# First head of the expert lookup scored by halves inside query unit 1, its first eight row numbers ahead of the rest, query units 2 to 4 unsplit

## The chip, the cores and the metric

One core of a Trainium2 chip runs the whole program. The metric is the device time of one execution in microseconds (us); smaller is better. The engines are TensorE (PE in the profile, with PEld for its weight loads), VectorE (DVE), ScalarE (ACT), GpSimd (POOL) and SyncE (SP); 16 DMA engines move the data.

## What is computed

Two transformer blocks over 256 tokens of width 1024, all in float32. The change lies in the last part, a feed-forward layer whose experts are looked up (PEER):

```python
def peer_ffn(x, w_q, sub_keys, u, v):
    def block(xb):                                   # 128 tokens
        q = (xb @ w_q).reshape(PEER_BLOCK, PEER_HEADS, 2, PEER_HALF)   # 8 heads, 2 halves of 128
        scores = jnp.einsum('thpd,hpkd->thpk', q, sub_keys).astype(jnp.float32)
        top_s, top_i = lax.top_k(scores, PEER_TOPK)  # 16 of 128 keys, for each half
        cand_s = (top_s[:, :, 0, :, None] + top_s[:, :, 1, None, :]).reshape(...)      # 16 x 16 sums
        cand_i = (top_i[:, :, 0, :, None] * PEER_N_KEYS + top_i[:, :, 1, None, :]).reshape(...)
        best_s, best_pos = lax.top_k(cand_s, PEER_TOPK)
        expert = jnp.take_along_axis(cand_i, best_pos, axis=-1)
        gate = jax.nn.softmax(best_s, axis=-1)
        act = jax.nn.gelu(jnp.einsum('thkd,td->thk', u[expert], xb).astype(jnp.float32), approximate=False)
        return jnp.einsum('thk,thkd->td', (gate * act).astype(v.dtype), v[expert])
```

## The kernel before

All matrices stream through nine raw buffers (`raw`, `RAW = 9`) in units of 128 x 1024 numbers, loaded by SyncE in a fixed order (line 572). A split unit is cut into a high part (`hi`, ScalarE, line 674) and a low part (`lo`, VectorE, line 1043), and TensorE multiplies each 128 x 128 piece three times (lines 548 to 550). Its raw buffer is free again after `lo`. A plain unit is multiplied as it lies in `raw` with the plain float32 activations `XF` (line 2269), and its buffer is free when TensorE has finished it. XF is written by ScalarE in eight copies, with one signal, `s_txf`, after the last (line 1015).

The order of the work on each engine is written out by hand, and each engine waits on semaphores. The lookup goes like this:

- TensorE forms the queries in 16 units `pq` 0 to 15, two for each head; ScalarE copies each to `QP` (line 1005). The units 0 to 4 are split, 5 to 15 plain. Units 0 to 15 lie in raw buffers 6, 7, 8, 0, 1, ..., 8, 0, 1, 2, 3, so unit 9 follows unit 0 in its buffer, unit 10 unit 1, and so on.
- A head's scores (line 2286: two halves times two token blocks, four matmuls, eight rows in the trace) follow a unit: head 0 after unit 1, head 1 after unit 4, head 2 after unit 6, and so on; ScalarE copies them to `SC` (line 1011).
- VectorE's `route` makes 16 row numbers of them for each token. `top16` (lines 1586 to 1593) is a search in five operations: the eight greatest, replace them, their places, the next eight, their places. It runs on both halves of 128 scores, then on the 256 sums (line 1608). Then shift, mask, convert (1616 to 1619), and for each half a comparison, a product and a sum over 256 elements (1621 to 1626) look up the key numbers; line 1629 writes the row numbers `EX`.
- GpSimd issues the gathers, one for each of 2 blocks x 8 heads x 16 (line 657). Gather g brings for each of the 128 tokens one row of 2048 numbers, the expert's u and v. It waits every 16 gathers for the head's row numbers (`s_exi`), for the landing of the gather 8 before (4 before, for the first 16), and for its buffer.
- There are 15 row buffers: four that are free early, then YH, YL, and halves of WH and WL (free after the last split unit), then pairs of raw buffers: 4-5 for the 11th gather (free after unit 8), 6-7 for the 15th (after unit 10), 0-1 for the 27th (after unit 13), and 2-3 and XF for the 35th and 36th (after unit 15). A used buffer is free again when TensorE has finished the slot of its gather.
- A slot: VectorE's dot product of u with the token (line 1669), ScalarE's gelu, gate and diagonal matrix (986 to 994), TensorE's product with v (line 2248, four rows in the trace). From unit 9 on, four slots follow each unit on TensorE (`MIX0 = 9`, `MIX = 4`); the other 228 follow unit 15.

Of the kernel before, what the change touches and what calls it, by code (L numbers as in the profile page):

```python
# [8 lines left out]
U32 = mybir.dt.uint32  # L9
# [5 lines left out]
T = 256  # L15
# [23 lines left out]
def plan():  # L39
# [97 lines left out]
    for t in range(16):  # L137
        add("pq", 1024, t < 5, lambda a, t=t: tile_b(a["peer_w_q_2"][0], ar(128) + 128 * t))
    return out
# [118 lines left out]
def program(nc, wst, cst, x, skt, uv, out, vscr, cscr, units):  # L258
    ctx = ExitStack()
    with ctx:  # L260
# [46 lines left out]
        def flat(ap):  # L307
# [130 lines left out]
        s_txf, s_xtt, s_qp, s_scm, s_scr = (sem(n) for n in ("x_gained", "x_turned", "pq_out", "pq_scores",  # L438
                                                                 "scores_out"))
        s_exi, s_bd, s_bde, s_gate, s_dot, s_gelu, s_wv, s_dg, s_y, s_ot, s_otd, s_left = (sem(n) for n in (  # L440
            "expert_index", "best_shifted", "best_exp", "gate", "dot", "gelu", "weight", "diag", "y_mm", "y_out", "y_out_right", "y_left_done"))
# [142 lines left out]
        def pool_program(po):  # L584
# [60 lines left out]
            for g in range(256):  # L645
                blk, s = g // 128, g % 128
                row, free, _ = rows[home[g]]
                if s % 16 == 0:
                    po.wait_ge(s_exi, g // 16 + 1)
                flying = FLYING // 2 if g < 2 * FLYING else FLYING  # L650
                if g >= flying:
                    po.wait_ge(s_g[home[g - flying]], 16 * turn_of[g - flying])
                if before[g] is None:
                    po.wait_ge(*free)
                else:
                    po.wait_ge(s_y, before[g] + 1)
                po.indirect_dma_start(row, None, uv if row.dtype == F32 else uv.bitcast(F32R), bass.IndirectOffsetOnAxis(ap=EX[:, blk, s:s + 1].bitcast(U32), axis=0)  # L657
                                      ).then_inc(s_g[home[g]], 16)


        def act_program(ac):
# [337 lines left out]
            for n in range(16):  # L999
# [3 lines left out]
                if n >= QN_RING:  # L1003
                    ac.wait_ge(s_scm, (n - QN_RING) // 2 + 1)
# [27 lines left out]
        def dve_program(dv):  # L1032
# [549 lines left out]

            lo("pq", 1)

            def top16(src, tmp, val, idx):
                own(dv.max(val[:, 0:8], src))
# [5 lines left out]
                own.wait()  # L1592
                own(dv.max_index(idx[:, 8:16], val[:, 8:16], tmp))

            def route(blk, h, step):
# [4 lines left out]
                if step < 2:  # L1600
                    n = 2 * h + step
                    dv.wait_ge(s_scr, 2 * h + blk + 1)
                    top16(SC[blk][:, n, :], SD[:, 0:128], TS[:, n, :], IX[:, n, :].bitcast(U32))
# [44 lines left out]

            for k in range(6):
                route(0, 0, k)  # L1650
            rstd(7)
# [26 lines left out]
        def pe_program(pe):  # L1678
# [5 lines left out]
            def gemm(name, n, off, nk, X, o, k0=0, x=None, first=True, last=True):  # L1684

                H, L = weights(name, n)
                for kc in range(nk):
                    if x:
                        pe.wait_ge(x[0], x[1] + kc + 1)
                    w = slice(off + 128 * kc, off + 128 * kc + 128)  # L1690
                    ins = three(pe, o, H[:, w], L[:, w], X[0][:, k0 + kc, :], X[1][:, k0 + kc, :], kc == 0, kc == nk - 1)
                return ins
# [549 lines left out]
            def slot(g):  # L2242
# [9 lines left out]
                ins.then_inc(s_y, 1)  # L2252

            for n in range(16):
                if n < 2:
# [3 lines left out]
                else:  # L2259
                    pe.wait_ge(s_qp, n - 1)  # L2260
                    for h in scored(n - 2):
                        pe.wait_ge(s_scr, 2 * h + 2)
                if n < SPLIT_PQ:
# [8 lines left out]
                if n == 1:  # L2272
                    pe.wait_ge(s_sk, 16)
                if n == 3:
                    pe.wait_ge(s_txf, 1)
                    for blk in range(2):
# [5 lines left out]
                for h in scored(n):  # L2282
                    pe.wait_ge(s_qp, 2 * h + 2)
                    for blk in range(2):
                        for i in range(2):
                            ins = pe.matmul(PS[:, bank_s[h], 256 * blk + 128 * i:256 * blk + 128 * i + 128],
                                            QP[:, (2 * h + i) % QN_RING, 128 * blk:128 * blk + 128],
                                            SK[:, 128 * (2 * h + i):128 * (2 * h + 1 + i)], start=True, stop=True,
                                            skip_group_check=True)
                    ins.then_inc(s_scm, 1)  # L2290
                if n == 1:
# [8 lines left out]
            for g in range(MIXED, 256):  # L2300
                if g == 64:
                    pe.wait_ge(s_scr, 16)
                    begin(1)
# [53 lines left out]
```

## Time and profile before

| what | value |
|---|---|
| median of 3 runs | 1894.38 us (1893.72 to 1896.72) |
| the profiled execution, first to last instruction | 1893.3 us |
| PE busy | 1751.9 us (93%) |
| DVE busy | 1294.2 us (68%) |
| ACT busy | 913.3 us (48%) |
| data moved by DMA | 485.02 MB, mean 256 GB/s |
| of it by gathers (q0, software_dynamic) | 275.25 MB |

The rows below are of one profiled execution. Times are us from its first instruction. A busy time is that in which an engine executes; a matmul's row overlaps the next one's, so the distance between starts tells the rate. A row of the timeline has start, duration, engine, line, operation, tensors written <- read, shapes and count, and in brackets the idle time of the engine before it and what ended it.

### The profile page before, as it was taken

What the parts mean: (1) busy time and instruction counts of PE and PEld (TensorE: products, weight loads), DVE (VectorE), ACT (ScalarE), POOL (GpSimd) and SP (SyncE); (2) the same over time, 40 slices, a digit from 0 to 9 for tenths busy, and PEclk for the clock granted to TensorE, in tenths of its full rate; (3) what the DMA queues carried; (4) which work ended last, traced back from release to release, by engine and by line L of the source; (5) the groups of instructions that cost most, each with busy time, mean ns of one, the idle gap of its engine ahead of it and who ended that gap; (6) DMA issues with size and microseconds to landing.
All of it is one profiled execution on the core that took longest, in us unless ns stands there. A gap on an engine that the chain in (4) does not pass through costs nothing.

```text
span 1893.3 us, 29213 instructions
## 1 busy us (share of the span) xinstructions
PE 1751.9 (93%) x11218; PEld 1390.2 (73%) x11218; DVE 1294.2 (68%) x2402; ACT 913.3 (48%) x1901; POOL 317.1 (17%) x332
## 2 busy tenths in 40 slices
PE   8999999999999999899999999999987777777777
PEld 8999979999999999679999889976332222232222
DVE  6565897555765575986656887885967766766444
ACT  5443665444544453665444665634544344344333
POOL 1000004000000000030000000433433333333331
PEclk9999999999999999999999999999999999999999
DMA  8555435975455545225555444699999999999997
GB/s 296 185 183 194 125 122 148 259 251 190 156 201 188 186 159 173 79 73 195 180 189 179 145 134 134 201 361 419 415 421 422 420 421 421 422 421 421 421 422 315
DMA packets 96138, 485.02 MB, mean 256 GB/s; under 512 B 10576, under 2 KB 10832, under 8 KB 62976
## 3 DMA queue, kind: packets, MB, share of 16 engines
q0 software_dynamic: 38544, 275.25, 37.7%
q1 hardware_dynamic: 57456, 207.90, 33.0%
q8 instruction: 90, 1.47, 0.3%
q14 instruction: 48, 0.39, 0.1%
HBM read 478.65 MB, written 4.46 MB: 255 GB/s over the span
## 4 chain that ended last, share of the span: by engine, by line
PE 59%; DMA 15%; issue 9%; DVE 8%; POOL 5%; ACT 3%; POOLq 0%; SPq 0%; ACTq 0%; DVEq 0%
PE PS L548 16%; PE PS L550 16%; PE PS L549 16%; PE PS L2248 4%; DMA raw<-uv,A 3%; DMA WH<-uv,A 2%; PE PS L2269 2%; DMA A<-uv,A 2%; DMA WL<-uv,A 2%; DMA raw<-wst 1%; DVE WL L1043 1%; POOL raw L657 1%; DMA XH<-uv,A 1%; DMA YL<-uv,A 1%; DMA XF<-uv,A 1%
## 5 line engine op out<-in xcount | busy, mean ns | idle before, releaser
L1043 DVE TENSOR_TENSOR WL<-raw,WH 128x1024 fp32r<-128x1024 f32 (+1 forms) x375 | 451.0, 1244 | 77.5 <-ACT WH L674 77.2
L548 PE MATMUL PS<-XH,WH 128*128 128x256 f32 x1616 | 458.4, 284 | 3.4 <-DVE XL L1051 1.9
L549 PE MATMUL PS<-XL,WH 128*128 128x256 f32 x1616 | 453.9, 281 | 0.0
L550 PE MATMUL PS<-XH,WL 128*128 128x256 f32 x1616 | 453.9, 281 | 0.0
L674 ACT ACTIVATE WH<-raw 128x1024 fp32r<-128x1024 f32 (+1 forms) x375 | 371.2, 1041 | 49.5 <-PE PS L550 26.6
L548 PEld LDWEIGHTS PS<-XH,WH 128*128 128x128 f32 x1616 | 304.0, 188 | 6.4 <-issue 3.3
L549 PEld LDWEIGHTS PS<-XL,WH 128*128 128x128 f32 x1616 | 304.1, 188 | 0.2
L550 PEld LDWEIGHTS PS<-XH,WL 128*128 128x128 f32 x1616 | 303.9, 188 | 0.0
L986 ACT ACTIVATE A<-A,RTK 128x1 f32<-128x1 f32 x256 | 75.0, 293 | 298.5 <-DVE A L1669 297.1
L727 ACT ACTIVATE A<-A 128x256 f32<-128x256 f32 x88 | 36.7, 418 | 343.0 <-DVE A L1078 343.0
L548 PE MATMUL PS<-GH,WH 128*128 128x256 f32 x704 | 198.2, 282 | 1.1 <-DVE WL L1043 1.1
L549 PE MATMUL PS<-GL,WH 128*128 128x256 f32 x704 | 197.8, 281 | 0.0
L550 PE MATMUL PS<-GH,WL 128*128 128x256 f32 x704 | 197.8, 281 | 0.0
L548 PE MATMUL PS<-YH,WH 128*128 128x256 f32 x584 | 165.6, 284 | 2.6 <-DVE WL L1043 1.9
L549 PE MATMUL PS<-YL,WH 128*128 128x256 f32 x584 | 164.1, 281 | 0.0
L550 PE MATMUL PS<-YH,WL 128*128 128x256 f32 x584 | 164.0, 281 | 0.0
L1078 DVE TENSOR_TENSOR A<-PS,RT 128x512 f32<-128x512 f32 x88 | 60.8, 691 | 142.6 <-PE PS L550 142.2
L2248 PE MATMUL PS<-raw,A 128*128 128x512 f32 x260 | 125.5, 609 | 30.0 <-ACT A L994 28.6
L548 PEld LDWEIGHTS PS<-GH,WH 128*128 128x128 f32 x704 | 132.6, 188 | 1.4 <-DVE WL L1043 1.3
L550 PEld LDWEIGHTS PS<-GH,WL 128*128 128x128 f32 x704 | 132.6, 188 | 0.0
L549 PEld LDWEIGHTS PS<-GL,WH 128*128 128x128 f32 x704 | 132.6, 188 | 0.0
L2248 PEld LDWEIGHTS PS<-raw,A 128*128 128x128 f32 x260 | 46.4, 191 | 106.2 <-issue 106.1
(317 smaller groups left out, 2947.0 us busy)
## 6 DMA issues: line engine op xcount, KB each, us to landing
raw<-wst SPq DMA_DIRECT2D x381, 512.0 KB, 4.6
raw<-wst SPq DMA_DIRECT2D x8, 384.0 KB, 3.4
vscr<-A POOLq DMA_DIRECT2D x1, 3072.0 KB, 37.0
A<-vscr POOLq DMA_DIRECT2D x1, 2048.0 KB, 22.7
C<-cst SPq DMA_DIRECT2D x1, 1236.5 KB, 11.5
raw<-uv,A POOLq DMA_INDIRECT x65
hT<-xin SPq DMA_DIRECT2D x2, 512.0 KB, 6.2
A<-vscr POOLq DMA_DIRECT2D x1, 1024.0 KB, 12.8
```

Source lines behind the costliest of these rows:

```text
L548: pe.matmul(o, wh, xh, start=start, stop=False, skip_group_check=True)
L549: pe.matmul(o, wh, xl, start=False, stop=False, skip_group_check=True)
L550: return pe.matmul(o, wl, xh, start=False, stop=stop, skip_group_check=True)
L657: po.indirect_dma_start(row, None, uv if row.dtype == F32 else uv.bitcast(F32R), bass.IndirectOffsetOnAxis(ap=EX[:, blk, s:s + 1].bitcast( ...
L674: ac.activation(WH[:, m % SPL, 0:w], raw[:, i % RAW, 0:w], ACT.Copy).then_inc(s_hi, 1)
L727: ac.activation(GS[:, b, 0, :], GS[:, b, 0, :], ACT.Silu).then_inc(s_silu, 1)
L986: own(ac.activation(AG[:, blk, s:s + 1], AV[:, blk, s:s + 1], ACT.Gelu, scale=RTK[:, blk:blk + 1]))
L1043: dv.tensor_tensor(WL[:, m % SPL, 0:w], raw[:, i % RAW, 0:w], f32(WH[:, m % SPL, 0:w]), ALU.subtract).then_inc(s_lo, 1)
L1078: dv.tensor_tensor(GS[:, b], PS[:, b, :].rearrange("p (a t) -> p a t", a=2), RT[:, 1:2, :].broadcast_to([128, 2, T]), ALU.mult).then_inc(s ...
L2248: ins = pe.matmul(PS[:, YB[blk] + q, :], DG[:, g % 4, :], v[:, 512 * q:512 * q + 512], start=False, stop=s == 127, skip_group_check=True)
L2269: ins = pe.matmul(PS[:, bank_q[n], 0:T], R[:, 128 * kc:128 * kc + 128], XF[:, kc, :], start=kc == 0, stop=kc == 7, skip_group_check=True)
```

## The change

- Units 2, 3 and 4 become plain: they are no longer split, are multiplied with XF, and unit 2 waits for XF (`s_txf`), which the turning of XF after unit 3 waited for before. The row buffers that waited for unit 4 wait for unit 1.
- Unit 1 is done in two halves of four pieces. Between them stand the scores of head 0's first half, which need only unit 0; those of its second half follow unit 1. They go to PSUM banks 2 and 3 (block 0) and 4 and 5 (block 1).
- VectorE reads block 0's scores of head 0 in PSUM (`first_route`); ScalarE copies only block 1's. The turning of XF, which writes those banks, waits for both readers (`first_scores_read`, `scores_out`).
- `first_route` forms the row numbers in two parts of eight, each with both key numbers in the same operations, and signals `expert_index` after each; GpSimd waits for the second signal ahead of the ninth gather.

```diff
-        add("pq", 1024, t < 5, lambda a, t=t: tile_b(a["peer_w_q_2"][0], ar(128) + 128 * t))
+        add("pq", 1024, t < 2, lambda a, t=t: tile_b(a["peer_w_q_2"][0], ar(128) + 128 * t))
...
-                if s % 16 == 0:
-                    po.wait_ge(s_exi, g // 16 + 1)
+                if g == 0:
+                    po.wait_ge(s_exi, 1)
+                elif g == 8:
+                    po.wait_ge(s_exi, 2)
+                elif s % 16 == 0:
+                    po.wait_ge(s_exi, g // 16 + 2)
...
-                if n == 0:
-                    hi("pq", 1)
                 for h in scored(n):
-                    ac.wait_ge(s_scm, h + 1)
+                    ac.wait_ge(s_scm, h + 2)
+                    if h == 0:
+                        ac.activation(SC[1][:, 0:2, :], PS[:, 4:6, 0:128], ACT.Copy).then_inc(s_scr, 1)
+                        continue
...
-            lo("pq", 1)
...
+            def first_route():
+
+                ix = IX[:, 0:2, :].bitcast(U32)
+                cs = flat(SC[0][:, 0:2, :])
+                bp = BP[:, 0, :].bitcast(U32)
+                dv.wait_ge(s_scm, 1)
+                top16(PS[:, 2, 0:128], SD[:, 0:128], TS[:, 0, :], ix[:, 0, :])
+                dv.wait_ge(s_scm, 2)
+                top16(PS[:, 3, 0:128], SD[:, 128:256], TS[:, 1, :], ix[:, 1, :], s_scd)
+                own.wait()
+                dv.wait_ge(s_scd, 1)
+                own(dv.tensor_tensor(cs.rearrange("p (i j) -> p i j", i=16), TS[:, 0, :].unsqueeze(2).broadcast_to([128, 16, 16]),
+                                     TS[:, 1, :].unsqueeze(1).broadcast_to([128, 16, 16]), ALU.add))
+                dv.tensor_copy(IXF[:, 0:2, :], ix)
+                own.wait()
+                own(dv.max(BS[:, 0, 0:8], cs))
+                own.wait()
+                own(dv.max_index(bp[:, 0:8], BS[:, 0, 0:8], cs))
+                a = own(dv.match_replace(SD, BS[:, 0, 0:8], cs, -3.0e38))
+                for n in range(2):
+                    k = slice(8 * n, 8 * n + 8)
+                    if n:
+                        own.wait(a)
+                        own(dv.max(BS[:, 0, k], SD))
+                        own.wait()
+                        own(dv.max_index(bp[:, k], BS[:, 0, k], SD))
...
+                    own(dv.tensor_tensor(c4, BF[:, :, k].unsqueeze(3).broadcast_to([128, 2, 8, 16]),
+                                         c("iota").unsqueeze(1).unsqueeze(1).broadcast_to([128, 2, 8, 16]), ALU.is_equal))
...
-            for k in range(6):
-                route(0, 0, k)
+            first_route()
             rstd(7)
...
+            def half_scores(h, i):
+
+                pe.wait_ge(s_qp, 2 * h + 2 if h else i + 1)
+                for blk in range(2):
+                    o = PS[:, bank_s[h], 256 * blk + 128 * i:256 * blk + 128 * i + 128] if h else PS[:, 2 + 2 * blk + i, 0:128]
+                    ins = pe.matmul(o, QP[:, (2 * h + i) % QN_RING, 128 * blk:128 * blk + 128],
+                                    SK[:, 128 * (2 * h + i):128 * (2 * h + 1 + i)], start=True, stop=True, skip_group_check=True)
+                return ins
...
+                if n == 1:
+                    pe.wait_ge(s_sk, 16)
+                    gemm("pq", 1, 0, 4, Y, PS[:, bank_q[1], 0:T], last=False)
+                    half_scores(0, 0).then_inc(s_scm, 1)
+                    gemm("pq", 1, 512, 4, Y, PS[:, bank_q[1], 0:T], k0=4, first=False).then_inc(s_used, 1)
+                elif n < SPLIT_PQ:
                     gemm("pq", n, 0, 8, Y, PS[:, bank_q[n], 0:T], x=(s_xl, 56) if n == 0 else None).then_inc(s_used, 1)
                 else:
                     R, sm, v = plain("pq", n)
                     pe.wait_ge(sm, v)
+                    if n == SPLIT_PQ:
+                        pe.wait_ge(s_txf, 1)
...
                 if n == 3:
-                    pe.wait_ge(s_txf, 1)
+                    pe.wait_ge(s_scr, 1)
+                    pe.wait_ge(s_scd, 1)
```

TensorE before, behind the last split piece of unit 1: head 0's scores (line 2286), the square sums (1716), and the first pieces of split unit 2. A name in brackets is the semaphore that a row waits for.

```order
L550 MATMUL PS<-YH,WL 128x256
L2286 MATMUL PS<-A 128x128 [waits pq_out,sub_keys]
L2286 MATMUL PS<-A 128x128 x3
L1716 MATMUL PS<-A,C 128x256 [waits x_squares]
L548 MATMUL PS<-YH,WH 128x256 [waits weight_low,pq_out]
```

TensorE after, at the same place: two matmuls of the second half's scores (line 2309), the square sums (1766), then units 2 and 3 plain (2336), the turning of XF (2345) and unit 4.

```order
L2309 MATMUL PS<-A 128x128 [waits pq_out]
L2309 MATMUL PS<-A 128x128
L1766 MATMUL PS<-A,C 128x256 [waits x_squares]
L2336 MATMUL PS<-XF,raw 128x256 [waits x_gained,raw_landed8,pq_out]
L2336 MATMUL PS<-XF,raw 128x256 x7
L2336 MATMUL PS<-XF,raw 128x256 [waits raw_landed0,pq_out]
L2336 MATMUL PS<-XF,raw 128x256 x7
L2345 MATMUL PS<-C,XF 128x128 [waits first_scores_read,scores_out]
```

What moved: unit 2 now waits for XF (`x_gained`) where it waited for its low part, and the turning comes behind two plain units.

ScalarE before, from the query copy of unit 0 (line 1005) on: a split copy (674), unit 1's query copy, two score copies (1011), the eight copies to XF (1015), the root.

```order
L1005 ACTIVATE A<-PS 128x256 [waits weight_used]
L674 ACTIVATE WH<-raw 128x1024 [waits weight_used,raw_landed1]
L1005 ACTIVATE A<-PS 128x256 [waits weight_used]
L1011 ACTIVATE A<-PS 128x256 [waits pq_scores]
L1011 ACTIVATE A<-PS 128x256
L1015 ACTIVATE XF<-hT,C 128x256 x8
L717 ACT_TABLE_LOAD
```

ScalarE after, at the same place.

```order
L1010 ACTIVATE A<-PS 128x256 [waits weight_used] x2
L1014 ACTIVATE A<-PS 128x256 [waits pq_scores]
L1021 ACTIVATE XF<-hT,C 128x256 x8
L722 ACT_TABLE_LOAD
L722 ACTIVATE RT<-PS,C 128x256 [waits square_sums]
```

What moved: the split copy and one score copy are gone, and the copies to XF still stand behind the score copy. On SyncE the last 15 weight loads were 13 that wait for a low part and 2 for a plain unit; they are now 10 and 5.

## Rows read from the trace of the kernel before

**Rows 1.** The page's slices: DMA share in tenths, and rate, 47.3 us each.

```profile
DMA  8555435975455545225555444699999999999997
GB/s 296 185 183 194 125 122 148 259 251 190 156 201 188 186 159 173 79 73 195 180 189 179 145 134 134 201 361 419 415 421 422 420 421 421 422 421 421 421 422 315
```

**Rows 2.** Stretches: length, PE, PEld, DVE, ACT, POOL busy, PEclk, DMA share, GB/s.

```profile
1227.00:1236.00 9.00, 9.00 (x78) 8.97 (x77) 8.14 (x25) 4.05 (x9) 1.43 (x2) 1.00 0.01 2
1236.00:1245.00 9.00, 9.00 (x48) 7.80 (x48) 7.72 (x34) 1.88 (x7) 4.36 (x5) 1.00 1.00 350
1236.00:1322.70 86.70, 86.23 (x333) 58.10 (x333) 59.39 (x170) 33.84 (x104) 30.63 (x33) 1.00 1.05 414
1323.00:1332.00 9.00, 7.60 (x22) 3.45 (x22) 5.94 (x18) 7.72 (x19) 6.87 (x8) 1.00 1.00 372
1224.25:1321.90 97.65, 97.65 (x430) 69.50 (x428) 69.81 (x207) 40.26 (x118) 32.06 (x34) 1.00 0.94 369
```

**Rows 3.** Timeline of POOL, issues of gathers: the 1st, 27th, 35th, and one later.

```profile
1234.27 1.06 POOL L657 DMA_INDIRECT XH<-uv,A  x1 [15.26 <-DVE A L1629]
...
1301.17 0.94 POOL L657 DMA_INDIRECT raw<-uv,A  x1 [5.94 <-PE PS L2269]
...
1322.70 0.94 POOL L657 DMA_INDIRECT raw<-uv,A  x1 [7.68 <-PE PS L2269]
...
1407.64 0.94 POOL L657 DMA_INDIRECT A<-uv,A  x1 [1.54 <-DMA XF<-uv,A]
```

**Rows 4.** Timeline of PE, first matmuls of scores, units 2, 4, 7 and others.

```profile
1223.04 1.13 PE L2286 MATMUL PS<-A 128*128 128x128 f32 x8 [0.57 <-ACT A L1005]
1224.00 0.60 PE L1716 MATMUL PS<-A,C 128*128 128x256 f32 x2
1224.25 0.47 PE L548 MATMUL PS<-YH,WH 128*128 128x256 f32 x1
...
1230.12 1.91 PE L2279 MATMUL PS<-C,XF 128*128 128x128 f32 x16
1231.79 0.36 PE L548 MATMUL PS<-YH,WH 128*128 128x256 f32 x1
...
1234.70 1.05 PE L2286 MATMUL PS<-A 128*128 128x128 f32 x8
...
1244.12 7.07 PE L2269 MATMUL PS<-XF,raw 128*128 128x256 f32 x32
1251.03 1.05 PE L2286 MATMUL PS<-A 128*128 128x128 f32 x8
...
1318.31 3.62 PE L2269 MATMUL PS<-XF,raw 128*128 128x256 f32 x16
```

**Rows 5.** Timeline of ACT, the eight copies to XF.

```profile
1224.75 3.30 ACT L1015 ACTIVATE XF<-hT,C 128x256 f32<-128x256 f32 x8
```

**Rows 6.** Timeline of DVE, steps of head 0's row numbers, block 0.

```profile
1226.08 0.28 DVE L1586 MAX8 A<-A 128x8 f32<-128x128 f32 x1
...
1227.64 0.18 DVE L1606 CAST A<-A 128x32 f32<-128x32 uint32 x1
...
1228.32 0.43 DVE L1586 MAX8 A<-A 128x8 f32<-128x256 f32 x1
...
1230.57 0.18 DVE L1616 TENSOR_SCALAR A<-A 128x16 uint32<-128x16 uint32 x1
...
1233.82 0.18 DVE L1629 SCALAR_TENSOR_TENSOR A<-A 128x16 uint32<-128x16 f32 x1
```

**Rows 7.** Stretches of PE alone: length, busy, PEclk, DMA share, GB/s.

```profile
1380.50:1383.90 3.40, 1.35 (x4) 1.00 1.01 422
1383.90:1387.30 3.40, 3.40 (x5) 0.50 1.02 424
```

**Rows 8.** Timeline of PE there: four slot matmuls at either clock.

```profile
1379.57 1.95 PE L2248 MATMUL PS<-XH,A 128*128 128x512 f32 x4 [0.52 <-ACT A L994]
1383.57 3.44 PE L2248 MATMUL PS<-XL,A 128*128 128x512 f32 x4 [2.05 <-ACT A L994]
```

**Rows 9.** Timeline of SP's queue, the last 16 weight loads issued.

```profile
1188.50 55.25 SPq L572 DMA_DIRECT2D raw<-wst  x16
```

More of the change, by code:

```diff
@@ L1581, in dve_program, with top16 @@
             project("wout", (6, 7, 0, 1) * 2, 7)
-            lo("pq", 1)
-            def top16(src, tmp, val, idx):
+            def top16(src, tmp, val, idx, read=None):
                 own(dv.max(val[:, 0:8], src))
@@ L1592, in top16 @@
                 own.wait()
-                own(dv.max_index(idx[:, 8:16], val[:, 8:16], tmp))
+                ins = dv.max_index(idx[:, 8:16], val[:, 8:16], tmp)
+                if read is None:
+                    own(ins)
+                else:
+                    ins.then_inc(read, 1)
+            def first_route():
[23 more added lines that the diff above has]
+                        own(dv.max_index(bp[:, k], BS[:, 0, k], SD))
+                    own.wait()
+                    own(dv.tensor_scalar(BI[:, 0, k].bitcast(U32), bp[:, k], 4, None, ALU.logical_shift_right))
+                    own(dv.tensor_scalar(BI[:, 1, k].bitcast(U32), bp[:, k], 15, None, ALU.bitwise_and))
+                    own.wait()
+                    own(dv.tensor_copy(BF[:, :, k], BI[:, :, k].bitcast(U32)))
+                    own.wait()
+                    c4 = cs.rearrange("p (q k j) -> p q k j", q=2, k=8)
+                    own(dv.tensor_tensor(c4, BF[:, :, k].unsqueeze(3).broadcast_to([128, 2, 8, 16]),
+                                         c("iota").unsqueeze(1).unsqueeze(1).broadcast_to([128, 2, 8, 16]), ALU.is_equal))
+                    own.wait()
+                    own(dv.tensor_tensor(c4, c4, IXF[:, 0:2, :].unsqueeze(2).broadcast_to([128, 2, 8, 16]), ALU.mult))
+                    own.wait()
+                    own(dv.tensor_reduce(EF[:, :, k], c4, AX, ALU.add))
+                    own.wait()
+                    dv.scalar_tensor_tensor(out=EX[:, 0, k].bitcast(U32), in0=EF[:, 0, k], scalar=128.0, in1=EF[:, 1, k],
+                                            op0=ALU.mult, op1=ALU.add).then_inc(s_exi, 1)
@@ L1690, in gemm @@
                     w = slice(off + 128 * kc, off + 128 * kc + 128)
-                    ins = three(pe, o, H[:, w], L[:, w], X[0][:, k0 + kc, :], X[1][:, k0 + kc, :], kc == 0, kc == nk - 1)
+                    ins = three(pe, o, H[:, w], L[:, w], X[0][:, k0 + kc, :], X[1][:, k0 + kc, :], first and kc == 0, last and kc == nk - 1)
                 return ins
@@ L2261, in pe_program @@
                     for h in scored(n - 2):
-                        pe.wait_ge(s_scr, 2 * h + 2)
-                if n < SPLIT_PQ:
+                        if h:
+                            pe.wait_ge(s_scr, 2 * h + 1)
+                if n == 1:
[4 more added lines that the diff above has]
+                elif n < SPLIT_PQ:
                     gemm("pq", n, 0, 8, Y, PS[:, bank_q[n], 0:T], x=(s_xl, 56) if n == 0 else None).then_inc(s_used, 1)
@@ L2282, in pe_program @@
                 for h in scored(n):
[L2283 to L2290, printed above, removed]
+                    if h:
+                        half_scores(h, 0)
+                    half_scores(h, 1).then_inc(s_scm, 1)
                 if n == 1:
@@ L2301, in pe_program @@
                 if g == 64:
-                    pe.wait_ge(s_scr, 16)
+                    pe.wait_ge(s_scr, 15)
                     begin(1)
```

7 lines of the change are left out of this document (3 added, 4 removed).

## The prediction, as written before the changed kernel ran

> **What bounds the kernel now.** I read the 40 slices first. From slice 26 on the DMA share stands at its ceiling and the transfers run at 415 to 422 GB/s to the end [rows 1]: this is the last stage, in which 256 gathers, one for each of the 16 rows of 8 heads and 2 token blocks, bring 128 rows of 8 KB each. One gather is 128 x 8192 B = 1.049 MB, at 421 GB/s 2.49 us, and 256 of them 638 us, a third of the span. In that stage each gather is issued when the one eight before it has landed: the wait at 1407.64 ends on a DMA [rows 3]. So the end of the kernel is the moment from which the gathers run without a break, plus what is left of them. Only two places can move it: where the stream starts, and where it breaks.
>
> Where it starts: for 9 us ahead of 1236 the DMA engines move nothing (2 GB/s) [rows 2], since the first gather, issued at 1234.27, waits for VectorE's first row numbers, the operation at 1233.82 [rows 3, 6]. It then takes a while to run full: 350 GB/s over the first 9 us from 1236 on [rows 2], 3.15 MB or 7.5 us at 422, as if the stream had begun in full at 1245 - 7.5 = 1237.5. That is 3.2 us after the issue; I call this the price of a start from empty.
>
> Where it breaks: TensorE is busy for all of the 97.65 us from 1224.25 to 1321.9 (PE busy equals the stretch) [rows 2]: query units, scores, and the slots of the first 28 gathers between them. It has no wait that could absorb a delay. Some gathers write into buffers that it must let go. The 27th is issued at 1301.17 after query unit 13 and the 35th at 1322.70 after unit 15, both released by the matmuls of line 2269 after 5.94 and 7.68 us of idle time of the issuing engine [rows 3, 4]. How full was the queue by then? From 1236 to 1322.7 it moved 86.7 us x 414 GB/s = 35.9 MB; two weight units of 0.52 MB each are in that, which leaves 34.85 MB or 33.2 gathers of the 34 issued. So 0.8 gather, 2.0 us, is left when the 35th is issued, and between 1323 and 1332 the rate falls to 372 GB/s [rows 2], a loss of 9 x 50 / 422 = 1.1 us. The stream is as good as dry there: 1322.7 + 2.0 + 1.1 = 1325.8, the same as the issue plus the price of a start from empty (1322.7 + 3.2 = 1325.9). **Today the end hangs on when TensorE finishes unit 15, not on when the first gather leaves.**
>
> **The change part by part.**
>
> *Row numbers of head 0.* Twelve matmuls of unit 1 go ahead of the first half-score, which costs the path of the second half four records of 0.12 us (8 took 0.96 from start to start) [rows 4]; the second half-score still ends at about 1224.2, as all four matmuls did (1223.04 + 1.13), since it is half as long. VectorE reads the scores in PSUM, without ScalarE's copy, and has the first top 16 behind it by then, since its scores come some 3 us sooner. Left after 1224.2: the second top 16, 1.56 (1226.08 to 1227.64); conversion and sum table, 0.68 (1227.64 to 1228.32); three of the five searches over 256 candidates, 1.35 of 2.25 (1228.32 to 1230.57); then of the 3.25 to 1233.82 half of the six passes over 256 elements falls away, since eight numbers of both coordinates go at once (1.38), leaving 1.87; and the last 0.18 [rows 6]. 1224.2 + 1.56 + 0.68 + 1.35 + 1.87 + 0.18 = 1229.85 against 1234.0: the first gather leaves 4.2 us earlier. Top 16 from PSUM has no row; I take the price from SBUF, bounds 0 and +1 us. Numbers 9 to 16 follow some 3 us later and are wanted only after eight gathers, about 20 us.
>
> *Weights of units 2 to 4 no longer split.* Three copies on ScalarE and three subtractions on VectorE go. None was waited for: TensorE ran on beside them, so they give nothing. But the raw buffers of these units are now let go by TensorE after each unit, at 1231 to 1241, not by VectorE before 1223. SyncE issues in order, so units 11 to 13 load behind that: the loads of the last 16 stretch today to 1243.8, the last two of them behind TensorE [rows 9]; after the change it is five. Three units of 0.52 MB, 3.7 us at 422 GB/s, move from the idle stretch into the gathers'. Of the 4.2 us, 0.5 is left once all weights are in.
>
> *TensorE.* This term decides. Unit 2 used to start at 1224.25 on split data [rows 4]. Unsplit it multiplies with XF, and ScalarE writes XF in eight copies from 1224.75 on, 3.30 us, with one signal at the end [rows 5]; one score copy instead of two lets them start 0.25 earlier, so they end at 1227.8. Unit 2 starts at 1227.85: **3.6 us of waiting** that were not there. Units 3 and 4, the turns, the scores of head 1 and all of the mixed units are queued behind it on TensorE, and behind them VectorE's second head and ScalarE's query copies. Then the units themselves: two split ones took 5.87 us (1224.25 to 1230.12), the third 2.91 (1231.79 after the turns of 1.67, to 1234.70); an unsplit one takes 3.46 (two in 6.91, 1244.12 to 1251.03) [rows 4]. 3 x 3.46 - 8.78 = **1.6 us more**.
>
> *The clock.* After an idle gap of 2.05 us, in a stretch in which TensorE was busy for 1.35 of 3.4 us, the granted clock stood at 0.50, the 1.2 GHz level, for 3.4 us, and four slot matmuls took 3.44 us where four others took 1.95 [rows 7, 8]. Not each such gap is followed by this, but none before 1321 is as long as the new one. At half clock 3.4 us lose 3.4 x (1 - 1.95 / 3.44) = 1.5; part of the low stretch falls into the idle time itself, so I take **1.2 us**, bounds 0 (no dip) and 3.0 (two such stretches). The Trainium skill, "TensorE: Matmul & The Clock Gate", Part 1, says the same: the gate lets half the pulses through by default, and only recent activity opens it. By that rule the dip comes; without it the sum below would be 5.2.
>
> *What of it reaches the end.* TensorE is late by 3.6 + 1.6 + 1.2 = 6.4 us through unit 15. The queue: with the 0.5 us gained, the 26 gathers before the 27th have moved by 1304.3 (today 1237.5 + 26 x 2.49 + 2.5 for the two weight units = 1304.8), but the 27th is issued at 1301.2 + 6.4 = 1307.6. The stream is dry for 3 us, restarts in effect at 1307.6 + 3.2 = 1310.8, and would be dry again after eight more at 1330.7. The 35th is issued at 1322.7 + 6.4 = 1329.1, with 1.6 us in the queue against 2.0 today, so it costs what it costs today: 1329.1 + 3.2 = 1332.3 against 1325.9. **+6.4 us**, and the earlier start is spent by the 27th. From there on all waits are on landings, and nothing gives back time. Bounds: 4.4, if the 2.0 us of queue hide that much, and 8.2 with the long dip. On the profiled execution: 1893.3 + 6.4 = 1899.7. The median of the runs stands 1.1 above its span, so 1894.4 + 6.4 = 1900.8.
>
> **The rivals.**
>
> *No dip of the clock.* For: several gaps of 2 us show none. Against: this gap is longer. 1894.4 + 5.2 = 1899.6.
>
> *A long dip.* For: no row excludes it. 1894.4 + 3.6 + 1.6 + 3.0 = 1902.6.
>
> *Part hidden.* If a gather needs less than 3.2 us to fill the stream once some of the last ones are in flight, up to 2.0 us go into the queue: +3.2 to +4.4, around 1898.
>
> *Faster: the start decides.* If the 35th gather's place in the stream is kept by the queue ahead of it, and the 27th likewise, the stream is one piece from its start, and the end moves with the start: 4.2 us less, 1890.2, or 0.5 less, 1893.9, with the three weight units counted. It decides if TensorE releases unit 15's buffer at least 3.2 us before the queue runs dry. For it speaks the idle DMA stretch of 9 us, which is real. Against: the 372 GB/s at 1323, where today's lead of 2.0 us was already too short, and the full 97.65 us [rows 2].
>
> *It doesn't do what it says.* The first gather does not leave earlier, because the second half's scores wait behind more than I count. The end is then still TensorE's: 1900.8, so this changes no number.
>
> **How the numbers follow.** The forecast as it stands 0.48, without a dip 0.22, long dip 0.11, part hidden 0.12 (half of it above 1898.2), the start decides 0.07 (mostly the 4.2). A measurement of this kernel can tell about 0.2%, 3.8 us, from no change: below 1890.6 faster, above 1898.2 slower. Slower 0.48 + 0.22 + 0.11 + 0.06 = 0.87; I take 0.80, since some small hold that I don't see may give way; same 0.13; faster 0.07. The range takes in the hidden case and the long dip: 1896.5 to 1903.0.
>
> **What would show it.** First gather issued at about 1230, DMA at work from 1232. TensorE idle for 3.6 us ahead of unit 2, released by ScalarE's XF; a granted clock of 0.5 in the next microseconds; the scores of head 1 starting some 6 us later than 1234.7; unit 15 ending at 1328, not 1321.9. Stretches far under 420 GB/s at about 1305 and 1330, and the 27th and 35th gathers still released by the query matmuls. Wrong it would be if TensorE made up its delay before unit 15, if the XF copies came earlier, or if the stream were full through 1330.

## The result, and the profile after the change

| | before | after |
|---|---|---|
| median (lowest to highest), us | 1895.62 (1893.72 to 1896.72), 5 runs | 1902.49 (1901.57 to 1905.55), 5 runs |
| ratio after / before, 95% interval | | 1.0042 (1.0031 to 1.0052) |
| profiled execution, first to last instruction | 1893.3 | 1899.8 |

The changed kernel is slower, by 8.0 us going by the ratio (0.0042 x 1895.6; its interval is 5.9 to 9.9 us). The forecast was 1900.8 us, 6.4 more than before, with a range of 1896.5 to 1903.0. The direction came out as forecast, and so did the path: TensorE's delay, the late 35th gather, the end. One term of the sum, the clock, was taken at less than half of what it cost in the profiled execution.

Now the trace, in the order of the forecast's steps. VectorE reads the half-scores in PSUM and writes the first eight row numbers at 1228.09 (`EX`, line 1643), the other eight 3.14 us later. The timeline of VectorE in the kernel after (start, duration, engine and line, operation, written <- read, in brackets the idle time before it and what ended it) answers to [rows 6]:

```profile
1220.13 0.30 DVE L1590 MAX8 A<-PS 128x8 f32<-128x128 f32 x1 [3.12 <-PE PS L2309]
...
1222.73 0.30 DVE L1590 MAX8 A<-PS 128x8 f32<-128x128 f32 x1 [1.05 <-PE PS L2309]
...
1228.09 0.17 DVE L1643 SCALAR_TENSOR_TENSOR A<-A 128x8 uint32<-128x8 f32 x1
...
1231.23 0.17 DVE L1643 SCALAR_TENSOR_TENSOR A<-A 128x8 uint32<-128x8 f32 x1
```

TensorE, next, answers to [rows 4]. Line 2309 is a half-score, line 2336 a plain query unit (16 rows), 2345 the turning of XF:

```profile
1221.98 0.71 PE L2309 MATMUL PS<-A 128*128 128x128 f32 x4 [0.47 <-ACT A L1010]
1222.53 0.60 PE L1766 MATMUL PS<-A,C 128*128 128x256 f32 x2
1226.44 9.67 PE L2336 MATMUL PS<-XF,raw 128*128 128x256 f32 x32 [3.31 <-ACT XF L1021]
1235.95 1.91 PE L2345 MATMUL PS<-C,XF 128*128 128x128 f32 x16
1237.69 3.62 PE L2336 MATMUL PS<-XF,raw 128*128 128x256 f32 x16
1241.15 1.05 PE L2309 MATMUL PS<-A 128*128 128x128 f32 x8
...
1324.76 3.62 PE L2336 MATMUL PS<-XF,raw 128*128 128x256 f32 x16
```

Units 2 and 3 stand behind an idle time of 3.31 us that ends with ScalarE's XF, whose copies run from 1223.01 to 1226.30:

```profile
1223.01 3.29 ACT L1021 ACTIVATE XF<-hT,C 128x256 f32<-128x256 f32 x8
```

From start to start these two units take 9.51 us (1226.44 to 1235.95), where two plain units took 6.91 before [rows 4]. The stretch view (length, busy time of PE, PEld, DVE, ACT, POOL with counts, then TensorE's granted clock, DMA share, GB/s) gives the reason in its clock column, 0.51, which is the 1.2 GHz level, against 1.00 behind it. TensorE works for 5.16 of these 6.90 us, and half of that is the 2.6 us that the two units take longer. The other stretches answer to [rows 2]:

```profile
1224.70:1231.60 6.90, 5.16 (x12) 4.21 (x13) 6.41 (x25) 3.35 (x6) 2.46 (x3) 0.51 0.16 39
1231.60:1240.00 8.40, 8.40 (x48) 7.55 (x48) 1.46 (x1) 0.77 (x2) 3.62 (x4) 1.00 1.02 375
...
1266.00:1272.00 6.00, 6.00 (x19) 3.24 (x18) 5.86 (x14) 1.85 (x7) 3.04 (x3) 1.00 0.74 233
...
1306.00:1311.00 5.00, 5.00 (x15) 2.50 (x15) 2.56 (x5) 3.86 (x13) 2.77 (x3) 1.00 0.61 208
...
1329.00:1338.00 9.00, 7.59 (x24) 3.69 (x25) 5.50 (x18) 7.30 (x18) 6.72 (x8) 1.00 0.92 328
```

Three stretches are far under the ceiling of 421 GB/s: at 1266, 1306 and 1329. GpSimd's timeline names the gather that came too late in each, and who held it: the 1st, 12th, 27th and 35th gathers, beside [rows 3]. The 12th waits for a slot on TensorE (line 2298), the 27th and 35th for a query unit (line 2336):

```profile
1228.53 1.06 POOL L662 DMA_INDIRECT XH<-uv,A  x1 [10.93 <-DVE A L1643]
...
1266.25 0.94 POOL L662 DMA_INDIRECT XH<-uv,A  x1 [6.89 <-PE PS L2298]
...
1307.62 0.94 POOL L662 DMA_INDIRECT raw<-uv,A  x1 [5.95 <-PE PS L2336]
...
1329.15 0.95 POOL L662 DMA_INDIRECT raw<-uv,A  x1 [7.68 <-PE PS L2336]
```

The first gather leaves 5.7 us earlier than before, the 35th 6.45 us later, and the end comes 6.5 us later: 570.7 us lie between the 35th and the end, 570.6 before. Two stretches, from the first gather's issue to the 35th's, tell how much was still queued then, after and then before:

```profile
1228.53:1329.15 100.62, 100.15 (x402) 70.37 (x402) 63.74 (x181) 35.22 (x107) 32.65 (x34) 0.98 0.98 377
...
1234.27:1322.70 88.43, 87.96 (x348) 59.81 (x347) 60.78 (x171) 34.43 (x105) 32.05 (x34) 1.00 1.03 406
```

After, 100.62 us x 377 GB/s are 37.93 MB, of which five weight units of 0.524 MB make 2.62; the other 35.31 MB leave 0.34 of the 35.65 MB of 34 gathers, 0.8 us at 421 GB/s. Before, 88.43 x 406 less two units leave 0.80 MB, 1.9 us. In the page's slices the dry places show as 396 and 404, where 419 and 415 stood before [rows 1]:

```profile
GB/s 295 190 178 197 129 113 150 261 250 193 161 204 177 193 145 181 69 91 188 189 187 162 162 133 134 175 378 396 404 420 422 422 421 422 422 421 421 421 421 314
```

### One origin for all traces

The program ahead of unit 1 isn't touched by the change, yet the profiled executions of all the kernels below come out of it at times that differ by up to 4 us. So times are counted below from **E**, the end of head 0's scores on TensorE: the last row of line 2286 before (1223.04 + 1.13 = 1224.17 in [rows 4]), the last half-score after (1221.98 + 0.71 = 1222.69). E lies inside the changed part, but the change hardly moves it: unit 1 starts 4.70 us ahead of E before and 4.62 us after. By this the profiled execution of after had a head start of 1.48 us that the change didn't give it.

| us from E | before | after | difference |
|---|---|---|---|
| first gather issued | 10.10 | 5.84 | -4.26 |
| unit 2 starts | 0.08 | 3.75 | +3.67 |
| unit 15 lets its buffer go (35th gather) | 98.53 | 106.46 | +7.93 |
| end of the span | 669.13 | 677.11 | +7.98 |

The +7.98 us at the end is also what the medians of the runs say, 8.0 (5.9 to 9.9).

### The profile page after: what moved, and what is told of

Read it like the earlier page. It is cut to its first block, busy times and chain, and to the rows that moved or that the text cites. A ratio compares the mean times of both kernels' runs of the same rounds, so it can differ in the third digit from the quotient of the medians.

```text
span 1899.8 us, 29160 instructions
## 1 busy us (share of the span) xinstructions
PE 1754.4 (92%) x11194; PEld 1390.8 (73%) x11194; DVE 1290.8 (68%) x2403; ACT 910.6 (48%) x1897; POOL 317.7 (17%) x332
## 4 chain that ended last, share of the span: by engine, by line
PE 59%; DMA 15%; issue 9%; DVE 8%; POOL 5%; ACT 3%; POOLq 0%; SPq 0%; ACTq 0%; DVEq 0%
PE PS L549 16%; PE PS L551 15%; PE PS L550 15%; PE PS L2298 4%; DMA raw<-uv,A 3%; PE PS L2336 3%; DMA XH<-uv,A 2%; DMA XF<-uv,A 2%; DMA YL<-uv,A 2%; DVE WL L1049 1%; DMA raw<-wst 1%; POOL raw L662 1%; DMA WH<-uv,A 1%; DMA A<-uv,A 1%; DMA WL<-uv,A 1%
## 5 line engine op out<-in xcount | busy, mean ns | idle before, releaser
L549 PE MATMUL PS<-YH,WH 128*128 128x256 f32 x560 | 158.6, 283 | 2.3 <-DVE WL L1049 1.5
L2298 PE MATMUL PS<-raw,A 128*128 128x512 f32 x260 | 131.0, 630 | 31.2 <-ACT A L999 31.1
L550 PE MATMUL PS<-YL,WH 128*128 128x256 f32 x560 | 157.3, 281 | 0.0
L551 PE MATMUL PS<-YH,WL 128*128 128x256 f32 x560 | 157.3, 281 | 0.0
```

The lines of the kernel that those rows point to most:

```text
L549: pe.matmul(o, wh, xh, start=start, stop=False, skip_group_check=True)
L550: pe.matmul(o, wh, xl, start=False, stop=False, skip_group_check=True)
L551: return pe.matmul(o, wl, xh, start=False, stop=stop, skip_group_check=True)
L2298: ins = pe.matmul(PS[:, YB[blk] + q, :], DG[:, g % 4, :], v[:, 512 * q:512 * q + 512], start=False, stop=s == 127, skip_group_check=True)
```

## The experiments

The theory is the forecast's: TensorE carries its delay to unit 15, the 35th gather waits for it, and the end follows at a fixed distance; the delay is the sum of a wait for XF, longer units and a dip of the clock. The main rival is that the start of the gathers, or the weight loads now among them, sets the end. All experiments compute the whole output. The table shows every kernel from E; "unit 15" is the issue of the gather that waits for it, the 35th, or in the kernels marked * the 37th. The ratios are to the kernel before in the same series.

| kernel | unit 15 | first gather | end of span | end, minus before | ratio (95%) | the same in us |
|---|---|---|---|---|---|---|
| before | 98.53 | 10.10 | 669.13 | | | |
| after | 106.46 | 5.84 | 677.11 | +8.0 | 1.0042 (1.0031 to 1.0052) | +8.0 |
| e1_split | 98.54 | 5.84 | 669.01 | -0.1 | 1.0001 (0.9992 to 1.0010) | +0.2 |
| e2_unsplit | 104.20 | 10.09 | 674.61 | +5.5 | 1.0045 (1.0031 to 1.0059) | +8.5 |
| e3_xf_early | 100.39 | 5.84 | 670.87 | +1.7 | 1.0010 (1.0001 to 1.0019) | +1.9 |
| e4_filler | 103.87 | 5.84 | 674.62 | +5.5 | 1.0030 (1.0019 to 1.0040) | +5.7 |
| e5_before_rows * | 98.54 | 10.10 | 668.55 | -0.6 | 0.9995 (0.9986 to 1.0004) | -0.9 |
| e6_split_rows * | 98.54 | 5.84 | 664.19 | -4.9 | 0.9977 (0.9968 to 0.9986) | -4.4 |
| e7_after_rows * | 105.63 | 5.85 | 671.24 | +2.1 | 1.0020 (1.0011 to 1.0029) | +3.8 |
| e8_xf_rows * | 100.38 | 5.85 | 666.53 | -2.6 | 0.9992 (0.9983 to 1.0001) | -1.5 |
| e9_split_xf_rows * | 98.55 | 5.85 | 664.15 | -5.0 | 0.9977 (0.9968 to 0.9986) | -4.4 |
| e10_split_rows_again * | 98.55 | 5.84 | 664.61 | -4.5 | 0.9976 (0.9967 to 0.9985) | -4.5 |

### Each half of the change alone

The new kernel with units 2 to 4 split again (e1). The two lines that put back the split copy on ScalarE and the one on VectorE are left out of the diff:

```diff
-        add("pq", 1024, t < 2, lambda a, t=t: tile_b(a["peer_w_q_2"][0], ar(128) + 128 * t))
+        add("pq", 1024, t < 5, lambda a, t=t: tile_b(a["peer_w_q_2"][0], ar(128) + 128 * t))
...
-                    if n == SPLIT_PQ:
-                        pe.wait_ge(s_txf, 1)
...
                 if n == 3:
+                    pe.wait_ge(s_txf, 1)
```

> The changed kernel with units 2 to 4 split as before; halves, PSUM reading and the eight early row numbers stay. TensorE's end decides (my theory): the first gather leaves some 4 us earlier than in the kernel before, TensorE finishes unit 15 when it did there (within 0.5 us, counted from the start of unit 1), so the end is that of the kernel before: difference 0, at most -1 us. Rival, the start of the gathers decides: -4 us against before. Rival, the new head 0 code itself is what costs: it stays near +7.

And the kernel before with only these three units plain (e2); here the same two lines go, which the diff leaves out too:

```diff
-        add("pq", 1024, t < 5, lambda a, t=t: tile_b(a["peer_w_q_2"][0], ar(128) + 128 * t))
+        add("pq", 1024, t < 2, lambda a, t=t: tile_b(a["peer_w_q_2"][0], ar(128) + 128 * t))
...
+                    if n == SPLIT_PQ:
+                        pe.wait_ge(s_txf, 1)
...
-                    pe.wait_ge(s_txf, 1)
```

> The kernel before with units 2 to 4 unsplit and nothing else. TensorE's end decides: unit 2 waits 3.8 us for XF, the units take 1.6 more, a low clock adds 1.2 to 2.6: +6.6 to +8 us, as much as the whole change. Rival, the three weight units that now load among the gathers are the price: +3.7 us. Rival, the halves and early numbers are what costs: 0.

Measured: e1 1895.06 us (1893.76 to 1897.05), e2 1902.88 us (1900.45 to 1904.98), the kernel before 1895.18 beside both. The whole loss is in the plain units, and the earlier first gather is worth nothing by itself. GpSimd's timeline of e1, the 1st, 27th and 35th gathers, shows where its 4.26 us go:

```profile
1229.53 1.06 POOL L662 DMA_INDIRECT XH<-uv,A  x1 [10.93 <-DVE A L1647]
...
1300.70 0.94 POOL L662 DMA_INDIRECT raw<-uv,A  x1 [5.94 <-PE PS L2338]
...
1322.23 0.94 POOL L662 DMA_INDIRECT raw<-uv,A  x1 [7.69 <-PE PS L2338]
```

The gathers start earlier and then wait for the same units at the same time from E (98.54 against 98.53). The stretches at these two places, of e1 and then of the kernel before:

```profile
1299.00:1306.00 7.00, 7.00 (x20) 3.51 (x19) 2.57 (x6) 3.91 (x13) 4.08 (x5) 1.00 0.73 265
...
1320.00:1332.00 12.00, 10.12 (x33) 5.23 (x32) 6.41 (x20) 8.54 (x21) 7.54 (x8) 1.00 0.96 363
```

```profile
1299.00:1306.00 7.00, 7.00 (x21) 3.74 (x20) 4.45 (x9) 3.90 (x13) 3.75 (x4) 1.00 1.05 418
1320.00:1332.00 12.00, 10.12 (x34) 5.39 (x34) 5.94 (x18) 8.10 (x20) 7.16 (x8) 1.00 1.02 386
```

265 GB/s at the 27th, where the kernel before had 418: 7 x 156 / 421 = 2.6 us of the stream lost there, and more at the 35th (363 against 386: 0.7 us). These two make 3.3 of the 4.26 us: the earlier start has become idle time of the DMA engines. This rules out the rival "the start decides".

### The wait for XF

The new kernel, with each piece of XF written by ScalarE as soon as the piece of `hT` is there, behind YH's; there is still one signal, after the last (e3):

```diff
                     if t:
                         high_x(p, t - 1)
+                        if p == 7:
+                            ac.activation(XF[:, t - 1, :], hT[:, t - 1, :], ACT.Copy, scale=c("gains", 63 + t, 64 + t))
...
                 if n == 1:
-                    for kc in range(8):
-                        ins = ac.activation(XF[:, kc, :], hT[:, kc, :], ACT.Copy, scale=c("gains", 64 + kc, 65 + kc))
-                    ins.then_inc(s_txf, 1)
                     root(7)
```

> The changed kernel with XF written one piece at a time behind each piece of YH, so that unit 2 finds it ready. The wait of 3.3 us and the low clock behind it go: TensorE is late by the unsplit units' 1.6 us alone, +1.6 us against before (+1 to +2). Rival, the weight loads decide: +3.7 less what the earlier start gives, 4.2, so -0.5. Rival, the wait is not what counts: still near +7.

Measured: 1896.91 us (1895.37 to 1897.94). TensorE's timeline of e3 around unit 2:

```profile
1224.32 0.71 PE L2310 MATMUL PS<-A 128*128 128x128 f32 x4 [0.47 <-ACT A L1014]
...
1225.30 7.07 PE L2337 MATMUL PS<-XF,raw 128*128 128x256 f32 x32
1232.21 1.91 PE L2346 MATMUL PS<-C,XF 128*128 128x128 f32 x16
```

No wait, no dip (two units in 6.91 us), and 6.07 of the 7.93 us are gone from unit 15's end. What is left is 1.86 us, of which 0.19 is unit 2's start (1225.30 - 1225.03 = 0.27 from E, against 0.08): the plain units cost 1.7 us. Of the loss, three quarters hung on where the XF copies stood in ScalarE's order.

### The clock apart from the wait

The new kernel with seven matmuls ahead of the wait for XF, which work on the sub-keys and which nobody reads (e4):

```diff
                     if n == SPLIT_PQ:
+                        for i in range(7):
+                            pe.matmul(PS[:, 6, 0:256], SK[:, 0:128], SK[:, 0:256], start=True, stop=True, skip_group_check=True)
                         pe.wait_ge(s_txf, 1)
```

> The changed kernel with seven unused float32 matmuls (3.0 us) on TensorE ahead of the wait for XF; their results are read by nobody. The wait for XF stays as long. If the granted clock falls because TensorE idles there, it stays at 1.00 and the end comes 2.6 us sooner than in the changed kernel's trace: +5.3 us against before. If the clock is not what costs, no change against the changed kernel: +7 to +8.

Measured: 1900.63 us (1898.82 to 1902.82). TensorE's timeline and the stretch over it:

```profile
1223.45 3.19 PE L2335 MATMUL PS<-A 128*128 128x256 f32 x14
1226.84 7.17 PE L2338 MATMUL PS<-XF,raw 128*128 128x256 f32 x32 [0.20 <-ACT XF L1021]
1233.85 1.91 PE L2347 MATMUL PS<-C,XF 128*128 128x128 f32 x16
```

```profile
1223.40:1231.60 8.20, 8.00 (x38) 6.72 (x37) 7.57 (x31) 5.52 (x12) 2.03 (x2) 1.00 0.09 18
```

Unit 2 starts 3.66 us from E, as in after (3.75), but the clock is 1.00 and two units take 7.01 us. From E the end comes 2.5 us earlier than in after, by the ratios 2.3 us. So between these two profiled executions the dip is worth 2.5 us at the end, and the wait the rest. By the runs alone this isn't clear of noise: the intervals of the two ratios overlap (1.0019 to 1.0040 and 1.0031 to 1.0052).

Three profiled executions have the wait with nothing in it: after's (3.31 us idle, low clock for 6.8 us), e7's (the same 3.31, 3.4 us low), and e2's (3.58 idle, none). TensorE in e2, and the stretch of e2, then TensorE and the stretch of e7:

```profile
1227.61 7.14 PE L2267 MATMUL PS<-XF,raw 128*128 128x256 f32 x32 [3.58 <-ACT XF L1013]
1234.59 1.91 PE L2276 MATMUL PS<-C,XF 128*128 128x128 f32 x16
```

```profile
1227.60:1231.60 4.00, 4.00 (x19) 3.54 (x20) 3.72 (x15) 1.90 (x3) 0.00 (x0) 1.00 0.00 0
```

```profile
1230.51 8.83 PE L2336 MATMUL PS<-XF,raw 128*128 128x256 f32 x32 [3.31 <-ACT XF L1021]
1239.18 1.91 PE L2345 MATMUL PS<-C,XF 128*128 128x128 f32 x16
```

```profile
1230.90:1234.50 3.60, 3.60 (x11) 2.87 (x10) 3.31 (x12) 1.24 (x2) 1.59 (x2) 0.53 0.15 18
```

In e2, e7 and after two units took 6.98, 8.67 and 9.51 us, which is 0.1, 1.8 and 2.6 us over the 6.91 of [rows 4]. The 0.1 is not the clock's, since e4 has it too at 1.00. In e7 all 3.4 us of low clock fell on work and cost 1.7; in after 5.2 of the 6.8 us did. Since e2 kept the clock at 1.00 with nothing in the wait, e4's one trace doesn't show that its seven matmuls kept it there; only its runs, with the overlap just named, speak for that. In e2 and e7 the profile thus shows less than the median does (+5.5 against +8.5, +2.1 against +3.8). I read this as other executions of these two having a longer dip than the profiled one. No trace of those executions exists, and they may as well have lost the time ahead of E, where the profiled ones differ by up to 4 us: this isn't shown. The Trainium skill, "TensorE: Matmul & The Clock Gate", Part 1, says of the slow matmuls at a kernel's start that their number varies between runs of one kernel, since the gate watches activity in a window that runs free of the program. The three traces agree with this in the middle of a kernel, with 0, 3.4 and 6.8 us; no run here shows such a window itself.

### Breaking the tie to unit 15

Two pairs of raw buffers and XF are taken two gathers later as row buffers, so that unit 15 holds the 37th gather, not the 35th. The same edit in the kernel before (e5), in e1 (e6), in after (e7) and in e3 (e8):

```diff
-            rows.append((flat(raw[:, 2 * k:2 * k + 2, :]), queried(n), early + MIX * max(n - MIX0, 0)))
-        rows += [(flat(XF[:, :, :]), queried(15), early + MIX * (15 - MIX0))]
+            rows.append((flat(raw[:, 2 * k:2 * k + 2, :]), queried(n), early + MIX * max(n - MIX0, 0) + 2 * (n > 10)))
+        rows += [(flat(XF[:, :, :]), queried(15), early + MIX * (15 - MIX0) + 2)]
```

> The kernel before with another order of row buffers and nothing else: raw pairs 0-1 and 2-3 and XF are taken up two gathers later (from the 29th, the 37th and the 38th on instead of the 27th, 35th and 36th), and the gathers that had them take buffers of slots that are done sooner. If the stream ran nearly dry at the 35th gather in the kernel before, the 1.1 us lost there come back: -1.1 us, no stretch under 410 GB/s around 1325. Rival, the stream was full there and the rate fell for another reason: 0.

> Units 2 to 4 split, early row numbers, and the later buffers. If what swallowed the earlier start was the wait of the 27th and the 35th gather for units 13 and 15, it now reaches the end: 4.7 us from the start and 1.1 from the dry place less some 0.5 at the 12th gather, -5 us against before. Rival, TensorE holds the stream by its slots in any case: -1 us at most.

> The changed kernel with the later buffers. TensorE is as late as in the changed kernel (6 to 8 us), but the stream depends on it at fewer places: it still runs dry at the 12th gather (2.9 us in the trace of the changed kernel), no more at the 27th and 35th (2.3 + 2.1): some 4.5 us less than the changed kernel, +2 to +3 against before. Rival, the delay comes through other slots: no gain, +7.

> The changed kernel with XF written early and the later buffers. The stream starts 4.5 us earlier, carries three weight units more (3.7 us), and is not held at the 27th and 35th gather: 1.1 + 4.5 - 3.7 = 1.9 less than before, -2 us. Here the moved weight loads have their price, which they had not in the changed kernel. Rival, they cost nothing even here: -5 us, as with the split units.

Measured: 1895.15, 1890.73, 1898.47 and 1893.23 us, the kernel before 1894.97 beside them. Of e6, GpSimd's 1st, 27th, 35th and 37th gathers, and the stretches at the two old places:

```profile
1228.75 1.06 POOL L662 DMA_INDIRECT XH<-uv,A  x1 [10.95 <-DVE A L1647]
...
1294.75 0.94 POOL L662 DMA_INDIRECT raw<-uv,A  x1 [0.78 <-PE PS L2302]
...
1314.55 0.94 POOL L662 DMA_INDIRECT WL<-uv,A  x1 [0.78 <-PE PS L2302]
...
1321.45 0.94 POOL L662 DMA_INDIRECT raw<-uv,A  x1 [4.23 <-PE PS L2338]
```

```profile
1299.00:1306.00 7.00, 7.00 (x18) 3.17 (x17) 3.79 (x7) 3.91 (x13) 3.76 (x4) 1.00 1.01 421
1306.00:1320.00 14.00, 14.00 (x55) 9.42 (x54) 1.23 (x2) 4.56 (x15) 3.75 (x4) 1.00 1.08 422
1320.00:1332.00 12.00, 10.12 (x32) 4.83 (x31) 7.16 (x24) 9.17 (x24) 6.05 (x7) 1.00 1.04 419
```

Unit 15 ends at the same time from E as before (98.54), the stream is full through it, and now the 4.26 us of earlier start arrive: 4.9 us from E, 4.4 by the ratio, faster than both kernels. In e5 the same edit without the earlier start brings at most 1 us and can't be told from nothing: there the start sets the end, at 658.45 us behind the first gather, as in e6 (658.35). So in the kernel before both limits lay within 1 us of each other, and to move either alone gives nothing. That is shown by the four kernels together: early start alone 0 (e1), later buffers alone 0 to -1 (e5), both -4.4 (e6).

e8 against e6 is the price of plain units that don't wait: the end is 2.3 us later from E, 2.9 by the medians of one series. The stretch of e8 from 1236 to 1345, over the 12th gather and unit 15 both:

```profile
1236.00:1345.00 109.00, 107.12 (x394) 68.55 (x393) 75.88 (x222) 47.56 (x140) 41.55 (x44) 1.00 1.06 420
```

The DMA engines of e8 are hardly ever short of work there, at 420 GB/s (e6: 418), though its 12th gather is issued 1.84 us later from E than e6's. So it isn't a late gather that costs e8 its 2.3 us, but more bytes: what the forecast called weight loads among the gathers. SyncE's queue from E on (start, duration until the last is issued) of e8, then of e6:

```profile
1228.19 17.51 SPq L573 DMA_DIRECT2D raw<-wst  x5
```

```profile
1237.99 4.51 SPq L573 DMA_DIRECT2D raw<-wst  x2
```

Three loads more are issued, five against two. About one of e8's five moves ahead of the gathers' data: from 1225 to 1231.9 the stream carries 80 GB/s, 0.55 MB, and the first gather's data follow. That leaves two more among the gathers, 2.5 us at 421 GB/s, near the 2.3 measured. e10, which is e6 again, ends at 664.61 from E where e6 has 664.19, so these differences hold to some 0.4 us.

In e7 the 12th gather, which in after did no harm, becomes the place that counts. GpSimd and the stretches of e7 from 1262 and 1329:

```profile
1269.48 0.94 POOL L662 DMA_INDIRECT XH<-uv,A  x1 [6.89 <-PE PS L2298]
```

```profile
1262.00:1268.00 6.00, 6.00 (x33) 5.00 (x33) 5.83 (x19) 4.50 (x13) 0.59 (x1) 1.00 1.06 425
1268.00:1274.00 6.00, 6.00 (x16) 2.73 (x15) 5.83 (x17) 3.02 (x10) 2.94 (x3) 1.00 0.67 227
1303.00:1310.00 7.00, 7.00 (x26) 4.65 (x25) 3.34 (x7) 1.16 (x4) 2.98 (x4) 1.00 1.07 421
1329.00:1338.00 9.00, 7.20 (x29) 4.28 (x27) 2.33 (x6) 4.98 (x10) 4.31 (x5) 1.00 1.05 418
```

The stream is full at 1303 and 1329, dry only at 1268, where TensorE's first mixed slots come late; 6 x 194 / 421 = 2.8 us are lost there. The later buffers don't help there. e7's end stands 628.52 us behind the issue of its 12th gather, e6's 628.55 behind its own: so e6 has next to no slack left at this place, and a TensorE that is 7 us late moves the end by 7 us through it (e7 against e6: 7.09 at unit 15, 7.05 at the end). The three weight loads, 3.7 us, are hidden under that delay.

### All three edits together

XF written early on top of e6 (e9), and e6 once more beside it (e10); the edits are those shown.

> This is the new kernel with query units 2 to 4 split again, the later row buffers and XF written piecewise behind YH: all three edits together. Theory (stream): with split units 2 to 4 no matmul stands behind the XF copies before the scores of unit 3, and with the later buffers the 35th gather does not wait for unit 15, so XF written early has nothing left to shorten: within 1 us of the kernel that has the first two edits alone (1890.7 us median there), its stretch from the first gather's issue to the end unchanged within 1 us. Rival (TensorE still sets the end): each us that TensorE gains before unit 3 is a us at the end, and the 3.3 us of XF copies come off: 1887.5 to 1889 us, with the 37th gather 2 to 3 us earlier than in that kernel, counted from the first scores.

> The kernel with units 2 to 4 split and the later row buffers once more, beside the one that also writes XF early, on the same chip. Every theory expects its ratio to the kernel before again near 0.9977 (0.9965 to 0.9990), that is 1890 to 1893 us; were its lead chance of one chip, it would come out within 0.2% of the kernel before.

Measured: 1890.55 us (1889.23 to 1893.12) and 1890.28 us (1889.08 to 1892.48), the kernel before 1895.39. The expectation of the stream theory held, that of TensorE as the limit fell: with split units behind head 0's scores nothing waits for XF, and writing it early changes unit 15's end by 0.01 us. e6's lead of 0.23% came out again as 0.24%.

## Why the forecast was right, and where it was off

- **Start of the gathers.** Forecast 4.2 us earlier, measured 4.26 from E (10.10 to 5.84). The prices from SBUF held in PSUM: a MAX8 over 128 scores takes 0.30 us there, 0.28 in SBUF [rows 6].
- **XF wait.** Forecast 3.6 us, measured 3.67 from E.
- **Unsplit units.** Forecast 1.6 us, measured 1.7 (e3).
- **Clock.** Forecast 1.2 us with bounds 0 to 3.0, measured 2.6 in the profile and 2.5 with the gap filled (e4). **This is the term that was mis-sized.** The step that failed took the one dip in [rows 7, 8], 3.4 us long, as the length, and then put part of it into the idle time. The profiled execution had two such stretches on end, 6.8 us; it is the rival "a long dip", which was sized at 3.0, with a chance of 0.11; all that was said for it was that no row excludes it. A dip of 6.8 us stood in the trace of the kernel before (behind this list). The forecast treated the dip as one number, while traces of this same wait show 0, 3.4 and 6.8 us, the last two in e7 and after, which run the same instructions up to there. The sum 3.67 + 1.7 + 2.6 = 8.0 closes on the 7.93 measured.
- **What of it reaches the end.** Forecast: all, at 3.2 us behind the 35th issue whatever is left in the queue. Measured: the end stands 570.4 to 570.8 us behind that issue in all six kernels with the old buffers, though it moved by up to 7.9 us. The rival "part hidden" falls with that. The queue itself was overrated: 0.8 us were left in it, not 1.6 (before: 1.9, where the forecast had 2.0), and this changed nothing at the end.
- **The 27th and 35th gathers** were forecast at 1307.6 and 1329.1 and issued at 1307.62 and 1329.15, and the span at 1899.7 against 1899.8. This agreement is partly luck: the profiled execution reached E 1.48 us early, and that made up for the 1.4 us missing from the clock. Counted from E the forecast was 1.5 us short.
- **The median.** 1902.49 is 1.7 us over the forecast. The comparison's kernel before ran at 1895.62, 1.2 above the 1894.38 on which the sum stood; by the ratio the shortfall is 8.0 - 6.4 = 1.6. That is the clock's size, but the forecast's 6.4 lies inside the ratio's interval (5.9 to 9.9), so the runs alone don't show a shortfall; the trace does.
- **The 12th gather** wasn't seen: it ran the stream dry for some 3 us at 1266. It cost nothing, since the 27th and 35th reset the stream behind it, but e7 shows that it would be the next limit.
- **Weights unsplit.** Forecast 3.7 us moved in among the gathers. Hidden in after. Where TensorE doesn't hide it (e8), 2.3 us: three loads came later there too, but one of them still moved ahead of the gathers.

The long dip in the trace of the kernel before, with waits of TensorE of 0.98 and 1.65 us that end at 774.32 and 776.90 (length, TensorE busy, clock, DMA share, GB/s):

```profile
776.30:783.10 6.80, 6.20 (x30) 0.50 0.01 2
```

## What to carry to other kernels

Where a stream of transfers has two limits within 1 us of each other, here its start and the release of a late buffer by another engine, neither edit alone shows its worth: an early start gained 0, and 4.4 us once the buffer had a later turn. Before work is made cheaper by feeding it from another tensor, look when that tensor is signalled: of 8 us lost here, 6 were one wait for the last of eight copies and the clock behind it. And compare traces from an event inside the part that the change touches, since what runs before it differs by more than the terms that are to be read.

## What the runs showed of the hardware

- The same idle time of TensorE, 3.3 to 3.6 us, was followed by 0, 3.4 or 6.8 us at 1.2 GHz in three executions; two units of 6.91 us took 0.1, 1.8 and 2.6 us longer. With fourteen matmul rows in that gap (e4) the clock stood at 1.00 in the one execution profiled; e2 had 1.00 without them.
- From the issue of the late 35th gather to the end lie 570.4 to 570.8 us in six kernels. With 1.9 us of gathers still queued at that issue (before) it was no shorter than with 0.8 us (after). Why the queue doesn't help isn't shown.
- The first 1220 us of the program, where after and e7 don't differ, end 4 us apart in their profiled executions (E at 1222.69 and 1226.76), and this carries through to the end. In after the clock stands at 1.00 all the way to E. In e7 it stands at 0.50 for 6.8 us from 746.2 and again at half for 3.4 us from 780.3, with TensorE busy throughout; half of the 10.2 us is 5.1, of the size of the 4.1 us between the two.
